# Gate stage: bias row in TensorE, weight remainders on VectorE, branches gated in pairs and summed on GpSimd

## What is computed

```python
h = layer_norm(x, ln_in_g, ln_in_b)
(pool_v, fq, fk, fv, ff, dq, dk, dv, iq, ik, iw, conv_in, gate) = split_columns(h @ w_in[l])
br_a = pool_mixer(...)            # causal means over 2, 4, 8, 16 tokens
br_b = fox_attention(...)         # 4 heads, causal, forget bias
br_c = dsa_attention(...)         # 4 heads over the 64 keys with the highest index score
br_d = conv_module(...)           # depthwise causal convolution, 31 taps, LayerNorm, silu
up = jnp.einsum('bsnc,ncd->bsnd', branches, w_branch[l])
g = jax.nn.sigmoid(gate.reshape(B, S, N_BRANCH, D) + b_gate[l].reshape(N_BRANCH, D))
mixed = jnp.sum(g * up, axis=2) @ w_out[l]
h = layer_norm(DEEPNORM_ALPHA * h + mixed, ln1_g[l], ln1_b[l])
moe = hier_moe(h, ...)            # 16 experts, 1024 -> 512 -> 1024, top 2 of one group of 4
h = layer_norm(DEEPNORM_ALPHA * h + moe, ln2_g[l], ln2_b[l])
```

## Time and profile before

| what | value |
|---|---|
| device time, 3 runs | median 515.64 us (514.35 to 516.59) |
| profiled execution: time, span | 511.86 us, 510.1 us |
| TensorE busy | 459.7 us, 90% |
| VectorE busy | 282.9 us, 55% |
| ScalarE busy | 157.3 us, 31% |
| GpSimd busy | 166.9 us, 33% |
| read from memory | 141.54 MB |

### The profile page before, as it was taken

One profiled execution on the slowest core, in us unless ns is written; L12 is line 12 of the kernel. 1 busy time (PEld: TensorE's weight loads), 2 busy tenths in 40 slices (PEclk: granted clock), 3 DMA queues, 4 the chain that ended last, 5 costly groups with the idle time before them and its releaser, 6 DMA issues.

```text
span 510.1 us, 6098 instructions
## 1 busy us (share of the span) xinstructions
PE 459.7 (90%) x2374; PEld 293.7 (58%) x2374; DVE 282.9 (55%) x488; ACT 157.3 (31%) x240; POOL 166.9 (33%) x96
## 2 busy tenths in 40 slices
PE   8999999997979889788888999999999999897870
PEld 8889998875767667557665433543444344432330
DVE  5089978998999997994454222123211322031247
ACT  3268256445072469323253000101021101000020
POOL 8856807299255836966150000000000000000002
PEclk9999999997979989999988999999999999999995
DMA  8991355545540566739972999999999999999922
GB/s 259 297 347 48 121 187 186 187 164 186 199 172 21 186 241 231 269 120 350 390 294 68 377 409 411 407 409 408 410 409 409 409 411 409 409 410 410 409 86 82
DMA packets 52408, 142.92 MB, mean 280 GB/s; under 512 B 6776, under 2 KB 11009, under 8 KB 52384
## 3 DMA queue, kind: packets, MB, share of 16 engines
q1 hardware_dynamic: 51152, 140.29, 72.8%
q10 hardware_dynamic: 752, 2.11, 1.2%
q0 software_dynamic: 480, 0.20, 0.3%
HBM read 141.54 MB, written 1.05 MB: 280 GB/s over the span
## 4 chain that ended last, share of the span: by engine, by line
DVE 39%; PE 27%; SPq 23%; DMA 4%; ACT 3%; issue 3%; POOL 0%; DVEq 0%; POOLq 0%
SPq L443 23%; PE bank L1352 8%; DVE ring L1593 7%; DVE rounded L1514 4%; PE bank L1375 4%; DVE work L1694 4%; PE bank L1220 4%; DMA ring<-in_expert_w_down_dram 4%; PE bank L1290 2%; PE bank L976 2%; PE bank L941 2%; DVE ring L1691 2%; DVE ln1p L1551 2%; DVE rounded L1642 2%; DVE score L1505 1%
## 5 line engine op out<-in xcount | busy, mean ns | idle before, releaser
L1352 PE MATMUL bank<-ring,gates 128*64 128x512 f32 x512 | 114.4, 598 | 6.6 <-DMA ring<-in_expert_w_up_dram 4.4
L1094 PE MATMUL bank<-rounded 128*128 128x512 f32 x384 | 98.1, 415 | 5.4 <-POOL rounded L606 3.6
L1094 PEld LDWEIGHTS bank<-rounded 128*128 128x128 f32 x384 | 75.6, 200 | 24.1 <-issue 4.7
L1352 PEld LDWEIGHTS bank<-ring,gates 128*64 128x64 f32 x512 | 35.7, 138 | 76.8 <-issue 65.3
L644 POOL TENSOR_TENSOR work<-work,ln1p 128x512 f32<-128x512 f32 x1 | 1.3, 1321 | 239.6 <-ACT work L931 239.6
L1375 PE MATMUL bank<-ring,gates 128*64 128x512 f32 x256 | 58.2, 598 | 1.3 <-DMA ring<-in_expert_w_down_dram 1.3
L1872 DVE SCALAR_TENSOR_TENSOR gates<-gates,bank 128x512 f32<-128x512 f32 x8 | 6.0, 748 | 81.5 <-PE bank L1352 81.5
L606 POOL TENSOR_TENSOR rounded<-ring,rounded 128x1024 fp32r<-128x1024 f32 x16 | 39.8, 2516 | 30.1 <-ACT rounded L738 30.1
L614 POOL TENSOR_TENSOR gates<-gates,ring 128x1024 f32<-128x1024 f32 x8 | 32.0, 4001 | 34.7 <-ACT gates L781 34.7
L1883 DVE TENSOR_TENSOR rounded<-bank,rounded 128x512 fp32r<-128x512 f32 x16 | 11.1, 692 | 53.6 <-ACT rounded L922 42.2
L1375 PEld LDWEIGHTS bank<-ring,gates 128*64 128x64 f32 x256 | 17.0, 136 | 35.3 <-issue 28.7
(11 more groups left out here) (254 smaller groups left out, 642.2 us busy)
## 6 DMA issues: line engine op xcount, KB each, us to landing
ring<-in_expert_w_down_dram SPq DMA_DIRECT2D x32, 1024.0 KB, 18.3
ring<-in_expert_w_up_dram SPq DMA_DIRECT2D x32, 1024.0 KB, 18.2
ring<-in_expert_w_gate_dram SPq DMA_DIRECT2D x32, 1024.0 KB, 17.7
ring<-in_w_in_dram SPq DMA_DIRECT2D x10, 2048.0 KB, 8.1
ring<-in_w_branch_dram SPq DMA_DIRECT2D x2, 2048.0 KB, 8.8
ring<-in_w_out_dram SPq DMA_DIRECT2D x2, 2048.0 KB, 10.6
ring<-in_w_in_dram SPq DMA_DIRECT2D x3, 1024.0 KB, 14.0
ring<-in_b_gate_dram SPq DMA_DIRECT2D x8, 256.0 KB, 4.6
```

What stands on the lines that cost most here:

```text
L1094: last = pe.matmul(bank[:, b, :], hT_part[hpart][:, k, b * P:(b + 1) * P], w[wpart][:, k, :], start=(k == 0 and hpart == wpart), stop=(k = ...
L1352: last = pe.matmul(bank[CAP * e:CAP * e + CAP, part // 2, :], xg[:, FC * h + k, c:c + CAP], w[:, e, k // 2, k % 2 * HALF:(k % 2 + 1) * HAL ...
```

## The change

- **Gate bias.** It is loaded once as 8 rows, split in high and rest (`bias_parts`, 40 rows with a gap), and added by one more matmul at the head of each `gate(t, b)`, with a column of 0s and 1s (`bias_pick`) as weights. `gate_bias` and its eight broadcast loads are gone. For tiles 4 to 7 ScalarE applies the sigmoid as it empties the bank; for tiles 0 to 3 it still copies first.
- **Remainders.** All eight tiles' rests, both halves of `w_branch` and all of `w_out` are made by VectorE. ScalarE makes the high part of `w_branch`'s first half, and the high parts of the attention branches straight from the bank.
- **Order on VectorE.** `fox(1)` ahead of `probs(0)`, `select(1)` behind both, taps in other portions; `1/count` is computed for 16 positions instead of 256.
- **Merging.** VectorE multiplies two branches in one instruction (`gated`, counted by `s_mixp`), and GpSimd makes all the additions (counted by `s_mix`).
- **Output projection.** The first half of the channels is done for all four blocks, then the second half. `w_out`'s second high part lies in slot 4, so slots 2 and 5 are fetched for the experts after `s_up` 16, slots 0 and 4 after `s_o` 4.
- **Tail.** VectorE makes all of LayerNorm 2, in four half rows; ScalarE's queue issues two of four stores.

```diff
@@ gpsimd
-            for t in range(0, 8, 2):
-                tile_rest(t + 1)
-                gate_bias(t)
-                gate_bias(t + 1)
...
+            i = 0
+            for dq in range(2):
+                for t in range(TB):
+                    o = work[:, t, dq * HALF:(dq + 1) * HALF]
+                    for pair in range(NB // 2):
+                        i += 2
+                        pool.wait_ge(s_mixp, i)
+                        if pair == 0:
+                            pool.tensor_tensor(o, gated[0][:, 0], gated[0][:, 1], ALU.add).then_inc(s_mix, 2)
+                        else:
+                            link(pool.tensor_tensor(gated[1][:, 0], gated[1][:, 0], gated[1][:, 1], ALU.add))
+                            pool.tensor_tensor(o, o, gated[1][:, 0], ALU.add).then_inc(s_mix, 2)
@@ scalar
             def gate_out(t, b):
+
                 act.wait_ge(s_gate, 2 * t + b + 1)
...
+                if t < NB:
+                    act.activation(gate_rows(t, b), bank[:, b, :], ACT.Copy).then_inc(s_gout, 1)
+                else:
+                    act.activation(gate_rows(t, b), bank[:, b, :], ACT.Sigmoid).then_inc(s_gsig[1], 1)
...
+            loaded(act, "wb0")
+            act.wait_ge(s_gate, 14)
+            for q in range(4):
+                c = slice(q * QUARTER, (q + 1) * QUARTER)
+                act.activation(rounded[WB_PART[0][0]][:, c], ring[:, SLOT["wb0"], c], ACT.Copy)\
+                    .then_inc(s_wbhi, 1)
@@ tensor, gate(t, b)
+                pe.matmul(bank[:, b, :], bias_pick[:, t:t + 1].broadcast_to([BIAS_ROWS, P]), bias_parts,
+                          start=True, stop=False)
...
-                        pe.wait_ge(s_lo[t % 2], 4 * (t // 2) + k // 2 + 1)
+                        pe.wait_ge(s_lo, 4 * t + k // 2 + 1)
@@ tensor, branch projections
                         if i < 2:
-                            pe.wait_ge(s_gout, 16)
+                            pe.wait_ge(s_gsig[1], 8)
...
                         if i >= 4:
-                            pe.wait_ge(s_mix, i - 3)
+                            pe.wait_ge(s_mixp, i - 3)
...
-            out_part(0, 0, 0, KC // 2)
+            for t in range(TB):
+                out_part(0, t, 0, KC // 2)
             turn_merged(2)
-            out_part(0, 1, 0, KC // 2)
             turn_merged(3)
             for t in range(TB):
-                out_part(0, t, KC // 2, KC)
-            for t in range(TB):
-                out_part(1, t, 0, KC)
+                out_part(1, t, 0, KC // 2)
+            for j in range(2):
+                for t in range(TB):
+                    out_part(j, t, KC // 2, KC)
@@ vector, merging
+                    for pair in range(NB // 2):
+                        nb = 2 * pair
+                        dve.wait_ge(s_up, i + 2)
+                        dve.wait_ge(s_gsig[dq], nb + 2 if dq == 0 else 2 * nb + 4)
+                        if i >= NB:
+                            dve.wait_ge(s_mix, i - 2)
+                        dve.tensor_tensor(gated[pair][:, :, :], bank[:, i % 4:i % 4 + 2, :], g[:, t, nb:nb + 2, :],
+                                          ALU.mult).then_inc(s_mixp, 2)
+                        i += 2
+                        dve.wait_ge(s_mixp, i)
+                        if i <= NB:
+                            branch_weights_rest(1, i - 2)
+                            branch_weights_rest(1, i - 1)
+                        if i == 3 * NB:
+                            out_weights_rest(0, 0)
+                            out_weights_rest(0, 1)
+                        if i == 4 * NB - 2:
+                            merged_rest(0)
+                            merged_rest(1)
```

More of the change, by code:

```diff
@@ L144, in hybrid_trunk_kernel @@
         work = sb("work", [P, TB, D])
-        bgate = early(3, [2, HALF])
+        bias_at = place[3]
+        early(3, [2, HALF])
+        pick_at = place[3]
+        early(3, [8])
+        BIAS_ROWS = 40
+        bgate = xflat[0:8, bias_at:bias_at + HALF]
+        bias_parts = rounded[SLOTS][0:BIAS_ROWS, bias_at + HALF:bias_at + 2 * HALF]
+        bias_pick = rounded[SLOTS][0:BIAS_ROWS, pick_at:pick_at + 8]
         vrows = early(0, [P], NROW)
@@ L254, in hybrid_trunk_kernel @@
         s_lnp = sem("ln_params_loaded")
-        s_bg = [sem(f"bgate{i}_loaded") for i in range(2)]
+        s_bg = sem("gate_bias_loaded")
         s_brlo = sem("branch_split")
@@ L490, in _ @@
                     .then_inc(s_slot[SLOT[f"wo{j}"]], 16)
[L492 to L494 removed]
+            sp.wait_ge(*USED["wb1"])
+            for e in (2, 5):
+                load_part(sp, e, 0, e)
             sp.wait_ge(s_mix, 4 * NB)
@@ L501, in _ @@
             sp.wait_ge(s_o, 4)
-            for e in (0, 5):
+            for e in (0, 4):
                 load_part(sp, e, 0, e)
@@ L639, in _ @@
                 affine(t, work, ln1p, s_h1)
-            pool.wait_ge(s_lnp, 96)
-            pool.wait_ge(s_zlast, 1)
-            o = work[:, 1, HALF:D]
-            link(pool.tensor_tensor(o, o, ln1p[:, 0, HALF:D], ALU.mult))
-            pool.tensor_tensor(o, o, ln1p[:, 1, HALF:D], ALU.add).then_inc(s_fin2, 1)
         @block.scalar
@@ L671, in _ @@
             act.dma_start(bforget[:, :], a["b_forget"][0].partition_broadcast(P)).then_inc(s_bf, 16)
+            for q in range(2):
+                act.dma_start(bgate[NB * q:NB * q + NB, :], a["b_gate"][0].rearrange("(n q c) -> q n c", n=NB, q=2)[q])\
+                    .then_inc(s_bg, 16)
             root(0)
@@ L859, in _ @@
                     .then_inc(s_wbhi, 1)
-            for t in range(4, 8):
-                sig(t)
             def merged_rounded(i):
@@ L929, in _ @@
             root(1)
-            act.wait_ge(s_shift, 1)
-            act.activation(work[:, 1, HALF:D], acc[:, 1, HALF:D], ACT.Identity, bias=mv[:, 1, 5:6],
-                           scale=mv[:, 1, 4:5]).then_inc(s_zlast, 1)
+            for t in range(TB):
+                act.wait_ge(s_fin, 2 * t + 2)
+                act.dma_start(out_v[:, t, HALF:D], work[:, t, HALF:D]).then_inc(s_out, 16)
         @block.tensor
@@ L1526, in _ @@
             select(0)
-            link(dve.reciprocal(rcnt[:, :, :], rcnt[:, :, :]))
             dve.wait_ge(s_vT, 2)
```

213 lines of the change are left out of this document (98 added, 115 removed).

## The result

| | before | changed |
|---|---|---|
| device time, median of the runs made side by side | 515.00 us (510.72 to 516.59, 4 runs) | 495.38 us (495.31 to 497.06, 4 runs) |
| profiled execution: time, span | 511.86, 510.1 us | 497.06, 495.3 us |
| TensorE, VectorE, GpSimd busy | 90%, 55%, 33% | 93%, 51%, 16% |

The ratio is 0.964, 95% interval 0.9577 to 0.9702. The forecast of 497 us is met. But it is met by two numbers that are not the same: between the two traces lie 14.8 us where 19.0 were worked out, and between the medians 19.6.

What follows compares the result with a forecast made beforehand. Expert loop bound by its 395 GB/s stream; earlier, TensorE's waits for VectorE, stretched by GpSimd. -13.7 - 4.5 - 0.8 = -19.0 from 511.86 gives 492.9, plus 3.8 to the median 496.7, said 497; 8 in 10: 490 to 508.

Steps and rivals of the forecast that it cites:

- gate stage: From 77.25 us to the first branch projection: that projection starts at about 182.3 instead of 195.97, -13.7 us.
- merge stage: Branch projections and `w_out`: of 9.1 us of TensorE waits, 4.6 stay through VectorE-GpSimd collisions, so -4.5 us.
- tail: End of the kernel: VectorE's eight instructions and a reciprocal end at 506.4, last store earlier, -0.8 us.
- Waits and slow blocks of the gate stage: Gate stage: TensorE's waits vanish, -11.4 us, and the three slow matmul blocks after them regain full clock, -7.2.
- the 0.8 from my dating: Gate stage: extra gain of 0.8 us from dating the queues, with the other small matmul blocks clean too.
- Bias matmuls: Gate stage: sixteen added matmuls at 0.233 us each cost +3.8 us, at most +6.4.
- Handover: Gate to merge stage: first projection waits for the last sigmoid behind ScalarE's table loads, +1.9 us (0.8 to 3).
- Rival 1: Merge stage gives nothing because collisions cost what fewer instructions save: -14.5 us, 501 us; chance 0.17.
- Which of `out_part`'s blocks ends last does not change; the residuals of the first half hide as before: Output projection at the merge stage's end: its new order was given no cost of its own.
- Expert parts: Expert loop: changed slot fetches arrive in time, cost 0, 3 to 5 us in hand; TensorE enters at 254.
- The step to the median: From profiled execution to median: 492.9 us plus the 3.8 by which the earlier median exceeded its profile, 496.7.
- The prediction's sentence on one SBUF input: Merge stage: VectorE instructions with at most one SBUF input are exempt from contention, so only the rests pay.

Runs made afterwards that it cites:

- e1: The changed kernel without the sixteen bias matmuls, so the gates get no bias: 489.48 us, ratio 0.951.
- e4: The changed kernel with 42 unused 128x512 additions from SBUF on GpSimd in the gate stage: 525.92 us, ratio 1.023.
- e5: The kernel before without GpSimd's gate bias addition and its eight loads, odd rests still on GpSimd: 499.88 us, ratio 0.971.
- e10: The changed kernel with 128-row bias matmuls, output projection block by block, and the last gate's sigmoid ahead of the convolution's silu: 489.29 us, ratio 0.949.
- e2: The changed kernel with the bias matmul's weights padded with zeros from 40 to 128 rows: 493.51 us, ratio 0.959.
- e8: The changed kernel with the merge stage's twelve additions on VectorE instead of GpSimd, pairs kept: 496.68 us, ratio 0.965.
- e7: The changed kernel with the second halves of the output projection block by block, residuals and slot 1 and 3 fetches following: 494.85 us, ratio 0.962.
- e3: The changed kernel with the rests of the four odd gate tiles back on GpSimd: 495.70 us, ratio 0.964.
- e6: The changed kernel with the second index selection back where it stood before, ahead of the taps: 495.69 us, ratio 0.963.

## Why the prediction was right, and where it was not

The trace's 14.8 us against the 19.0 worked out, all dates from the rows above and the earlier trace rows:

| term | predicted | measured in the traces |
|---|---|---|
| gate stage (first projection 195.97 to 185.83) | -13.7 | -10.1 |
| merge stage (55.69 to 50.18) | -4.5 | -5.5 |
| last `w_out` matmul to first expert matmul (20.7 to 22.2) | 0 | +1.5 |
| expert loop to the first reciprocal of the tail | 0 | +0.5 |
| tail (9.8 to 8.7) | -0.8 | -1.1 |
| sum (of the unrounded terms) | -19.0 | -14.8 |

- **Waits and slow blocks of the gate stage: right.** Without the bias matmuls (e1) TensorE ends the gates at 176.35 instead of 195.97 - 1.05 = 194.92: 18.6 us. The terms for waits and clock come to 11.4 - 1.05 + 7.2 = 17.6, and 18.4 with the 0.8 from my dating. e4 and e5 show the cause, GpSimd's activity. One reading was wrong: the 1.05 us at the end of the stage before was not for VectorE, which was done at 195.64, but for ScalarE's copy of the last bank, done at 195.76. A wait of this kind stays in every kernel (0.84 in e10), and the handover's term holds it.
- **Bias matmuls: mis-sized.** "I take 3.8", with 6.4 as the upper bound; it was 8.2, outside of both. I priced one at the spacing of full ones, and above at a matmul and a load that does not overlap; but with 40 rows each costs 0.51 net, with 128 rows 0.19 (e1, e2), so that the price I took would have been near for full ones. This is the largest error, 4.4 us.
- **Handover: right in kind, late in date.** The sigmoid was late behind ScalarE's table loads, and the wait 1.25 where I said 1.9. That TensorE came 4 us later from the dearer bias matmuls hid part of it: in e2, nearer to my dates, it was 2.01. What I did not price is what such a wait leads to: behind 2.0 us the next 36 matmuls take 10.0, behind 1.25 they take 8.44.
- **Merge stage: right.** I foresaw waits of 0.6 and 2.1 behind the second and third multiplication and 4.6 in all; they are 0.67 and 1.70, and 3.5 in TensorE's rows, where before they were 7.8 (not the 9.1 that I took; the other 1.3 of the 5.5 is busy time of TensorE, 47.9 to 46.7). But the reason is thinner than I put it: GpSimd's additions do not carry it (e8). What is left are the multiplications in pairs, the remainders that GpSimd no longer makes and the order of the output projection, and no run parts these. Rival 1, that the stage gives nothing, did not come.
- **"Which of `out_part`'s blocks ends last does not change; the residuals of the first half hide as before": true, but not worth 0.** The last block is the same, but the last two end nearer together, so the normalisation of block 0 no longer hides behind `w_out` (e7). The second turning starts 4.76 us behind the last `w_out` matmul, before 3.96. That is 0.8 of the 1.5 us; the rest comes further on, where the granted clock of the whole step is 0.82 and was 0.87.
- **Expert parts, tail: right.** The loop starts at 258.22, 14.1 earlier than before, at 395 GB/s again; its first used slot is fetched anew at 263.12 instead of 276.71. No wait for slot 0.
- **The step to the median.** I took before's profiled execution as 3.8 us under its median and added as much to mine. Over its 29 other runs, those beside the experiments included, before lies between 510.4 and 517.1, most of them above 512.9, and the profiled one, 511.9, is near the fast end. The changed kernel lies between 495.3 and 497.1, and its profiled execution is the slowest of four; the others have spans of 493.6. So 1.7 us come off where I added 3.8, which makes up 5.5 us: 496.7 + 4.2 (the terms) - 5.5 = 495.4. The number was right by 1.6 us because two errors of 4 to 6 us cancel, and that is luck. What spreads before's runs over 6 us no run here shows. Like waits did bring the lower clock in one run and not in another: behind 3.40 us for VectorE in the merge stage twelve matmuls took 2.98 us before, behind the same wait of 3.41 in e5 4.59. But that this makes the spread is argued, not shown, and e4, which waits more, spreads only 0.95.

Of the reasons, I named GpSimd's whole activity as the cause. The runs say which part of it: the addition of the bias, 15.1 us (e5). It acted in at least two ways that e5 does not part: it stretched VectorE's instructions (e4 shows that way by itself), and it stood in GpSimd's queue ahead of the odd rests for which TensorE waited. The rests of the odd tiles could have stayed (e3) and so could the selection (e6).

## What to carry to other kernels

Ask of an engine that is off the critical path what its activity costs its neighbour: here deleting one group of GpSimd instructions with its loads, whose results were needed late, gave 15 us. When a small operation with an odd shape is put into a dense stream of another engine, measure its spacing and try it padded to full shape. After an engine has been freed, look at the next handover first: nearly half of what e2 won there (2.4 of 5.2 us) was taken back by one activation that stood behind another's table loads.

## What the runs showed of the hardware

- A matmul of 512 columns with 40 rows of weights among full ones: 0.43 us to the next start and 0.51 net; with 128 rows 0.24 and 0.19. More rows were cheaper, by 5.2 us for sixteen.
- GpSimd gets little beside dense taps: in e5 four of its rests of 128x1024 took 17.7 us where thirty taps ran in 11.97, 0.40 each and not stretched. At a later tile four took 10.0, and there four taps took 8.09; the mean of all taps was 583 ns, in the changed kernel 482. Both sides pay, and which of them pays more differs from place to place.
- Instructions with one tensor input from SBUF were stretched too: the scaling 128x256 from 350 to 1083 ns (e3), where the merge stage's multiplication with half its input in PSUM stayed at 1.22 us. The Trainium skill ("SBUF — State Buffer", Who interferes with whom) counts `tensor_scalar` and casts among the operations that can take the shared port pair; both lines behaved so, the cast of 128x512 with 2065 ns before and 430 now. The prediction's sentence on one SBUF input left this condition out; as it stands there, the scaling contradicts it.
- After a wait of 2.0 us the next 36 matmuls ran at a granted clock of 0.83 and took 10.0 us, after 1.25 or 0.84 at 1.00 and 8.44. At this place a wait shortened by 1.2 us was therefore worth 2.8 (e10). The length of the wait alone does not decide: in e8 24 matmuls behind a wait of 2.00 us in the merge stage ran at 1.00:

```profile
199.30 5.70 PE L1224 MATMUL bank<-rounded 128*128 128x512 f32 x24 [2.00 <-DVE ring L1697]
```
